# Recurrent mixer: chunk products as single 32x32 blocks in 32-row, 32-column tiles of the array

## The reference, cut to what matters

```python
def step(state, inp):
    r_t, w_t, k_t, v_t, kk_t, a_t = inp
    sa = jnp.einsum('bhvk,bhk->bhv', state, -kk_t)
    state = (state * w_t[:, :, None, :]
             + sa[..., None] * (kk_t * a_t)[:, :, None, :]
             + v_t[..., None] * k_t[:, :, None, :])
    y_t = jnp.einsum('bhvk,bhk->bhv', state, r_t)
    return state, y_t
```

## Time and profile before

| | us |
|---|---|
| median of 3 runs | 3006.22 |
| lowest, highest | 3001.57, 3009.12 |
| the profiled execution | 3007.8 |
| its span | 3006.0 |
| TensorE busy in it | 2891.0 (96%) |
| VectorE busy | 2076.3 (69%) |
| ScalarE busy | 1485.9 (49%) |

### The profile page before, as it was taken

How to read it: one execution, slowest core, us unless ns; L and a number is a source line. 1 busy time by engine, 2 the same in 40 slices (tenths; PEclk the granted TensorE clock), 3 DMA queues, 4 the chain that set the end, 5 groups by cost and what they waited for, 6 DMA issues and landing times.

```text
span 3006.0 us, 57317 instructions
## 1 busy us (share of the span) xinstructions
PE 2891.0 (96%) x24112; PEld 2684.4 (89%) x24112; DVE 2076.3 (69%) x3498; ACT 1485.9 (49%) x2406; POOL 291.1 (10%) x488
## 2 busy tenths in 40 slices
PE   6889999999999999999999998999999999999987
PEld 2578877889998899999899998999999999999987
DVE  6357777687788886756656657575988746887565
ACT  3335555365566646554443433545655444555454
POOL 0012222100133222100000011010000000000000
PEclk8799999999999999999999998999999999999999
DMA  9888877885755566554333333565555555555543
GB/s 388 314 266 265 267 262 242 300 287 176 199 174 166 169 203 196 183 172 156 117 121 118 122 115 118 165 197 183 163 183 185 187 185 179 184 183 188 177 161 113
DMA packets 168210, 580.79 MB, mean 193 GB/s; under 512 B 40273, under 2 KB 40305, under 8 KB 155537
## 3 DMA queue, kind: packets, MB, share of 16 engines
q1 hardware_dynamic: 146784, 525.40, 53.0%
q0 software_dynamic: 20592, 48.26, 5.3%
q10 hardware_dynamic: 576, 3.47, 0.3%
HBM read 555.22 MB, written 21.76 MB: 192 GB/s over the span
## 4 chain that ended last, share of the span: by engine, by line
PE 86%; DMA 5%; DVE 5%; ACT 1%; issue 1%; SPq 1%; POOL 1%; DVEq 0%; ACTq 0%
PE acc L1004 84%; DMA arena<-in_w_ada 2%; DVE arena L972 2%; PE acc L1007 2%; DVE rounded L972 1%; DMA scr_k<-arena 1%; SPq L969 1%; DMA upper<-in_w_ada 1%; DVE upper L972 1%; DVE upper L980 1%; DMA scr_u<-upper 0%; DMA arena<-scr_k 0%; DVE rounded L980 0%; ACT arena L1001 0%; POOL arena L969 0%
## 5 line engine op out<-in xcount | busy, mean ns | idle before, releaser
L1004 PE MATMUL acc<-rounded 128*128 128x256 f32 x14592 | 1883.6, 287 | 20.6 <-issue 9.0
L1004 PEld LDWEIGHTS acc<-rounded 128*128 128x128 f32 x14592 | 1795.7, 193 | 100.4 <-issue 83.0
L1001 ACT ACTIVATE rounded<-arena 128x1024 fp32r<-128x1024 f32 (+1 forms) x862 | 875.3, 1022 | 749.5 <-PE acc L1004 677.1
L972 DVE TENSOR_TENSOR rounded<-arena,rounded 128x1024 fp32r<-128x1024 f32 (+1 forms) x830 | 985.0, 1199 | 260.0 <-ACT rounded L1001 259.5
L1004 PEld LDWEIGHTS acc<-upper_rounded,rounded 128*128 128x128 f32 x4656 | 563.6, 193 | 18.0 <-issue 14.2
L1004 PE MATMUL acc<-upper_rounded,rounded 128*128 128x256 f32 x4656 | 570.2, 284 | 2.7 <-DVE rounded L972 2.0
L1001 ACT ACTIVATE arena<-arena 128x256 f32<-128x256 f32 (+3 forms) x473 | 233.0, 515 | 170.7 <-DVE arena L972 116.1
L972 DVE TENSOR_TENSOR arena<-acc,arena 128x256 f32<-128x256 f32 (+5 forms) x270 | 113.9, 432 | 238.1 <-PE acc L1004 237.3
L972 DVE TENSOR_TENSOR arena<-arena 128x256 f32<-128x256 f32 (+4 forms) x455 | 234.6, 526 | 36.9 <-ACT arena L1001 28.9
L1004 PE MATMUL acc<-arena 128*32 128x512 f32 (+7 forms) x1542 | 214.4, 486 | 39.3 <-DMA arena<-in_w_ada 24.8
L980 DVE SCALAR_TENSOR_TENSOR arena<-arena 128x256 f32<-128x256 f32 (+5 forms) x465 | 205.3, 446 | 29.9 <-ACT arena L1001 21.8
(11 more groups left out here) (92 smaller groups left out, 1212.4 us busy)
## 6 DMA issues: line engine op xcount, KB each, us to landing
arena<-in_w_in SPq DMA_DIRECT2D x328, 512.0 KB, 4.7
arena<-in_w_ada SPq DMA_DIRECT2D x88, 1024.0 KB, 5.2
arena<-in_w_up SPq DMA_DIRECT2D x176, 512.0 KB, 4.0
arena<-in_w_down SPq DMA_DIRECT2D x88, 512.0 KB, 3.8
arena<-in_w_outa SPq DMA_DIRECT2D x32, 512.0 KB, 5.6
arena<-in_w_glu SPq DMA_DIRECT2D x32, 512.0 KB, 5.4
arena<-in_w_outm SPq DMA_DIRECT2D x32, 512.0 KB, 4.8
arena<-in_w_out SPq DMA_DIRECT2D x32, 512.0 KB, 4.0
```

What stands on the lines that cost most here:

```text
L972: return self.put(self.e and self.e.tensor_tensor(o, a, b, op))
L1001: return self.put(self.e and self.e.activation(o, a, f, scale=scale, **kw))
L1004: return self.put(self.e and self.e.matmul(o, l, r, start=start, stop=stop, skip_group_check=True))
```

## The change

The masks shrink from 128 to 32 columns, and each unit's operand from 128 (or 192) columns to 32 (or 96): a chunk's rows stay on their own 32 partitions, and its block begins at column 0. Every product is then made block by block. A tile of 32 rows and 32 columns of the array takes a chunk's block of weights; four chunks of a unit lie on four such tiles along the diagonal.

```diff
-        def four(bank, l, r, n=128):
-            for u in range(4):
-                x = pe.mm(B(bank, 128 * u, n), V(l + 128 * u, 128), V(r + 128 * u, n), True, True)
+        def chunks():
+            return [(u, dict(p0=32 * r, np_=32)) for u in range(4) for r in range(4)]
+
+        def scores(bank, l, r, *dims):
+            for hf in range(2):
+                for c in range(4):
+                    for hd in range(2):
+                        at = 128 * hf + 32 * c
+                        x = pe.mm(B(bank + hd, 128 * hf, 32 * (1 if len(dims) == 1 else 2), p0=32 * c, np_=32),
+                                  V(l + at, 32, p0=64 * hd, np_=64), V(r + at, *dims, p0=64 * hd, np_=64), True, True)
             return x
 
-        def apply(bank, l, src):
-            for u in range(4):
-                x = pe.mm(B(bank, 256 * u, 192), V(l + 128 * u, 128), V(src + 192 * u, 192), True, True)
+        def four(bank, l, r):
+            for u, p in chunks():
+                x = pe.mm(B(bank, 32 * u, 32, **p), V(l + 32 * u, 32, **p), V(r + 32 * u, 32, **p), True, True)
+            return x
+
+        def apply(bank, l, step, src):
+            for u, p in chunks():
+                x = pe.mm(B(bank, 128 * u, 96, **p), V(l + step * u, 32, **p), V(src + 96 * u, 96, **p), True, True)
+            return x
+
+        def rows(at, n, l, step, r, step_r):
+            for hf in range(2):
+                for c in range(4):
+                    for hd in range(2):
+                        u, p = 2 * hd + hf, dict(p0=32 * c, np_=32)
+                        x = pe.mm(B(3 + c, at + 128 * hf, n, p0=64 * hd, np_=64), V(l + step * u, 64, **p),
+                                  V(r + step_r * u, n, **p), True, True)
             return x
```

Steps 4 and 5 use `scores` for `ab`, `ba` and `mrk` (16 products each, where there were 4). Steps 6 to 12 keep their calls of `four` and `apply`, now of 16 products each. In step 13 TensorE has:

```diff
-            for u, (hd, hf) in enumerate(U4):
-                x = pe.mm(B(7, 128 * hf, 128, p0=64 * hd, np_=64), V(QTT + 192 * u, 64), V(MBT + 192 * u, 128), True, True)
-            x.then_inc("rw_pe", ("g7", i))
-            for u in range(4):
-                x = pe.mm(B(4 + u // 2, 256 * (u % 2), 192), V(QTT + 192 * u + 64, 128), V(MBT + 192 * u, 192), True, True)
-            x.then_inc("rw_pe", ("hk", i))
-            for u, (hd, hf) in enumerate(U4):
-                x = pe.mm(B(3, 256 * hf, 256, p0=64 * hd, np_=64), V(QTT + 192 * u, 64), V(BTM + 256 * u, 256), True, True)
-            x.then_inc("rw_pe", ("f", i))
+            apply(7, QTT + 64, 96, MBT).then_inc("rw_pe", ("hk", i))
+            rows(0, 96, QTT, 96, MBT, 96).then_inc("rw_pe", ("gf", i))
```

and in step 14 `e` becomes `rows(0, 64, KE, 64, VTK, 64)`; `y` stays four products of 64-column weights, with its right side in a block-spread copy `MRW`. On ScalarE the moves out of PSUM shrink from 512 to 128 columns (steps 6 to 8) and from 768 to 384 (steps 10, 11). On VectorE:

```diff
-            dve.tt(V(BTM, (256, 4), (64, 4), (1, 64)), V(MBT + 128, (192, 4), (0, 4), (1, 64)),
-                   V(CON + CCOL["ch4"], (0, 4), (1, 4), (0, 64)), MUL)
...
-            dve.tt(V(EE, 512), V(EE, 512), B(5, 0, 512), ADD).then_inc("rw_dve", (e, i))
+            dve.tt(V(EE, 128), V(EE, 128), B(5, 0, 128), ADD).then_inc("rw_dve", (e, i))
...
-            dve.tt(V(QTT, 4, 192), V(QTT, 4, 192), B(3, 0, (256, 4), (1, 192)), ADD).then_inc("rw_dve", ("a3", i))
+            dve.tt(V(QTT, 4, 96), V(QTT, 4, 96), B(3, 0, (128, 4), (1, 96)), ADD).then_inc("rw_dve", ("a3", i))
...
-            dve.wait_ge("rw_pe", ("g7", i))
-            dve.tt(V(G + 256 * i, 256), B(7, 0, 256), V(Rf, 256), ADD)
             dve.wait_ge("rw_pe", ("hk", i))
-            dve.tt(f4(MRK), f4(MRK), quad(4, 0), ADD)
-            dve.wait_ge("rw_pe", ("f", i))
-            dve.tt(V(Bf, 8, 64), B(3, 0, 8, 64), V(CON + CCOL["id64"], (0, 8), (1, 64)), ADD)
+            dve.tt(V(MRK, 4, 32), V(MRK, 4, 32), B(7, 0, (128, 4), (1, 32)), ADD)
             dve.wait_ge("rw_act", ("kv", i))
-            dve.tt(V(KE, 4, 64), V(KTT, 4, 64), B(4, 128, (256, 4), (1, 64)), ADD)
-            dve.tt(V(BTM, (256, 4), (64, 4), (1, 64)), V(VTK, (64, 4), (0, 4), (1, 64)),
-                   V(CON + CCOL["ch4"], (0, 4), (1, 4), (0, 64)), MUL).then_inc("rw_dve", ("vm", i))
+            dve.tt(V(KE, 4, 64), V(KTT, 4, 64), B(7, 32, (128, 4), (1, 64)), ADD)
+            dve.settle()
+            dve.tt(V(MRW, 4, 4, 32), V(MRK, (32, 4), (0, 4), (1, 32)), V(CON + CCOL["ch4"], (0, 4), (1, 4), (0, 32)), MUL)
+            dve.wait_ge("rw_pe", ("gf", i))
+            dve.tt(V(G + 256 * i, 2, 4, 32), B(3, 0, (128, 2), (512, 4), (1, 32)), V(Rf, 2, 4, 32), ADD)
+            dve.tt(V(Bf, 2, 4, 64), B(3, 32, (128, 2), (512, 4), (1, 64)), V(CON + CCOL["id64"], (0, 2), (0, 4), (1, 64)),
+                   ADD).then_inc("rw_dve", ("vm", i))
```

More of the change, by code:

```diff
@@ L68, in const_array @@
     put("chk", np.where(t // 64 <= s // 64, 0, -1e30))
[L69 to L73, removed]
+    i, j = s % 32, np.arange(32)[None, :]
+    put("m16s", (i < j) & (i // 16 == j // 16))
+    put("mo", (i < j) & (i // 16 != j // 16))
+    put("m32i", i <= j)
+    put("m16t", (j < i) & (i // 16 == j // 16))
+    put("m32t", j < i)
+    put("i32", i == j)
     put("scm", np.broadcast_to(np.arange(256) % 32 != 0, (128, 256)))
@@ L121 @@
 CON = _c.alloc(NCON)
+ROOM = _c.alloc(448)
 COS = _c.alloc(256)
@@ L171 @@
 CQ, CQH = Q0T, BTM + 768
+MRW = BTM
 MPR, MPT, MSM, MNM = TMPS + 1024, TMPS + 1408, TMPS + 1792, TMPS + 1800
@@ L229, in mask4 @@
     def mask4(self, name):
-        return self.V(CON + CCOL[name], (0, 4), (1, 128))
+        return self.V(CON + CCOL[name], (0, 4), (1, 32))
     def HT(self, j):
@@ L1300, in rw @@
             pe.wait_ge("rw_dve", ("z", i))
-            for u, (hd, hf) in enumerate(U4):
-                x = pe.mm(B(3 + hd, 256 * hf, 256), half(Bf, hd, hf, 128), half(Af, hd, hf, (256, 2), (1, 128)), True, True)
-            x.then_inc("rw_pe", ("ab", i))
-            for u, (hd, hf) in enumerate(U4):
-                x = pe.mm(B(5 + hd, 256 * hf, 256), half(Af, hd, hf, 128), half(Bf, hd, hf, (256, 2), (1, 128)), True, True)
-            x.then_inc("rw_pe", ("ba", i))
+            scores(3, Bf, Af, (256, 2), (1, 32)).then_inc("rw_pe", ("ab", i))
+            scores(5, Af, Bf, (256, 2), (1, 32)).then_inc("rw_pe", ("ba", i))
             if i:
@@ L1319, in rw @@
             pe.wait_ge("rw_dve", ("m3", i))
-            for u, (hd, hf) in enumerate(U4):
-                x = pe.mm(B(3 + hd, 256 * hf, 128), half(Kf, hd, hf, 128), half(Rf, hd, hf, 128), True, True)
-            x.then_inc("rw_pe", ("mrk", i))
+            scores(3, Kf, Rf, 32).then_inc("rw_pe", ("mrk", i))
             pe.wait_ge("rw_act", ("bt", i))
@@ L1348, in rw @@
             pe.wait_ge("rw_dve", ("e3", i))
-            apply(3, EE, Q0T).then_inc("rw_pe", ("a1", i))
+            apply(3, EE, 32, Q0T).then_inc("rw_pe", ("a1", i))
         if s == 11:
             pe.wait_ge("rw_act", ("a1", i))
-            apply(5, OO, QTT).then_inc("rw_pe", ("a2", i))
+            apply(5, OO, 32, QTT).then_inc("rw_pe", ("a2", i))
         if s == 12:
             pe.wait_ge("rw_act", ("a2", i))
-            apply(3, EE, Q0T).then_inc("rw_pe", ("a3", i))
+            apply(3, EE, 32, Q0T).then_inc("rw_pe", ("a3", i))
         if s == 13:
@@ L1358, in rw @@
             pe.wait_ge("rw_act", ("kv", i))
-            for u, (hd, hf) in enumerate(U4):
-                x = pe.mm(B(7, 128 * hf, 128, p0=64 * hd, np_=64), V(QTT + 192 * u, 64), V(MBT + 192 * u, 128), True, True)
-            x.then_inc("rw_pe", ("g7", i))
-            for u in range(4):
-                x = pe.mm(B(4 + u // 2, 256 * (u % 2), 192), V(QTT + 192 * u + 64, 128), V(MBT + 192 * u, 192), True, True)
-            x.then_inc("rw_pe", ("hk", i))
-            for u, (hd, hf) in enumerate(U4):
-                x = pe.mm(B(3, 256 * hf, 256, p0=64 * hd, np_=64), V(QTT + 192 * u, 64), V(BTM + 256 * u, 256), True, True)
-            x.then_inc("rw_pe", ("f", i))
+            apply(7, QTT + 64, 96, MBT).then_inc("rw_pe", ("hk", i))
+            rows(0, 96, QTT, 96, MBT, 96).then_inc("rw_pe", ("gf", i))
         if s == 14:
             pe.wait_ge("rw_dve", ("vm", i))
+            rows(0, 64, KE, 64, VTK, 64).then_inc("rw_pe", ("e", i))
             for u, (hd, hf) in enumerate(U4):
[L1371 to L1374, removed]
+                x = pe.mm(B(7, 128 * hf, 128, p0=64 * hd, np_=64), V(VTK + 64 * u, 64), V(MRW + 128 * u, 128), True, True)
             x.then_inc("rw_pe", ("y", i))
@@ L2264, in rw @@
         Af, Bf = AR + 512 * i, BK + 512 * i
-        quad = lambda bank, off: B(bank, off, (256, 4), (1, 128))
-        f4 = lambda base: V(base, 4, 128)
+        quad = lambda bank, off: B(bank, off, (512, 2), (128, 2), (1, 32))
+        f4 = lambda base, step=32: V(base, (2 * step, 2), (step, 2), (1, 32))
+        mask = lambda name: V(CON + CCOL[name], (0, 2), (0, 2), (1, 32))
         if s == 1:
@@ L2299, in rw @@
             dve.wait_ge("rw_pe", ("ab", i))
[L2300 to L2302 removed]
+            dve.tt(f4(DD), quad(3, 0), mask("m16s"), MUL)
+            dve.tt(f4(OO), quad(3, 0), mask("mo"), MUL)
+            dve.tt(f4(MBT, 96), quad(3, 32), mask("m32i"), MUL).then_inc("rw_dve", ("m3", i))
             dve.wait_ge("rw_pe", ("ba", i))
[L2304 to L2307 removed]
```

(5 more changed lines are left out.)

33 lines of the change are left out of this document (11 added, 22 removed).

## The result

| | before | after |
|---|---|---|
| median, us | 3005.66 (3001.57 to 3009.12) | 2940.44 (2932.61 to 2943.78) |
| ratio, 95% interval | | 0.9783 [0.9769, 0.9796] |
| the profiled execution | 3007.8 | 2932.6 |
| its span | 3006.0 | 2930.8 |
| groups of the mixer begin every (mean of seven) | 51.40 | 43.76 |

The account below looks back on a forecast made before the run. TensorE was taken to bound the mixer. Waves 7.7, borders 4.0 and instruction supply 0.5 make 12.2 us a group against 19.0: 54 us for eight, 55 with step 10's wait, off 3007.8 gives 2953 us; range 2938 to 3014.

Parts of the forecast that it names:

- The bound: Mixer's eight groups: TensorE bounds them, so its savings come off the end one for one; VectorE's and ScalarE's hardly count.
- Step 10's old wait: Step 10 stands 0.27 us for step 9's VectorE addition; shorter additions mostly end it, worth 1 us over all groups.
- named signs of being wrong: Granted clock below 1.00 in the stage, borders far over 0.33 us, or VectorE or ScalarE waits at steps 5, 10, 14.
- The waves: Small-tile products of a group: 7.7 us in all, a four-tile wave of `four` at 0.045 us (0.031 to 0.062).
- Step 9: Step of one `four` call: 32 records, about 0.4 to 0.5 us from its start to the next dense record.
- The borders: Changes of tile shape: 0.33 us for each of eleven blocks a group, 0.2 for each change inside steps 13 and 14; 4.0.
- The supply of instructions: Bursts in the mixer that outrun the supply of instructions: 0.5 us a group (0 to 1.5).
- The sum: One mixer group falls from 19.0 to 12.2 us: 6.8 saved, 54 us for eight groups.
- this case's own low end: Whole kernel: low end of the main forecast's range, 2941 to 2972 us, from savings of 4.5 to 8.3 a group.
- Rival 1: `four` and `apply`: row tiles sharing a PSUM bank take turns, 5.9 us more a group, 3055 us; chance 0.12.
- Rival 2: Mixer's small tiles: each record costs a floor of 0.027 us whatever its size, no change, 3009 us; chance 0.13.
- Rival 3: Steps 6 to 12: instructions come too slowly, 0.024 us each, half the gain, 2980 us; chance 0.13.

Follow-up runs that it names:

- moves_twice: The changed kernel with every move out of PSUM in steps 4 to 13 on ScalarE and every masked multiply or addition on VectorE made twice: 2940.80 us.
- after_again: The changed kernel with nothing altered, measured again: 2941.35 us, ratio to before 0.9790.
- borders experiment: The changed kernel with four more whole-array products a group, between calls of `four` in steps 6, 7 and 8: 2947.99 us.
- own_banks: The changed kernel with step 9's four row tiles writing to four banks and VectorE's addition behind it split in four: 2951.32 us (one run).
- tile_order: The changed kernel with the loop turned so that `four` and `apply` issue one tile's four products in a row: 2995.34 us.
- double_four: The changed kernel with each product of `four` issued twice, 256 more records a group: 2998.34 us.
- phase: The changed kernel with 32 more 32x32 products (128 instructions) in step 0 of group 1: 2933.64 us (one run).
- merged_spread: The changed kernel with two dense slots moved from behind step 5 to behind steps 6 and 7, and `mrk` made in step 4: 2931.79 us.

## Why the prediction was right, and where it was off

**The bound.** Right. TensorE had the stage, its time came off the end one for one (62.2 of the 75 us between the profiled executions lie in the stage), and moves_twice puts back most of ScalarE's part and under half of VectorE's without any cost. No new wait came up at steps 5, 10 or 14. Step 10's old wait of 0.27 is gone in most groups; the 1 us for it is too small a term to tell. One of the named signs of being wrong did show, though not for the reason given: the granted clock fell in the stage of after_again, behind a gap and not because the tiles are small; in the profile of after it stayed at 1.00 through all of them.

**The waves.** Mis-sized. I took 0.045 us for a wave of `four`, halfway between 0.031 and 0.062. Step 9 takes 0.38, of which 8 x 0.033 = 0.26 are waves, and each further call in a block costs 0.30, 0.037 a wave. For 64 waves that is 2.2 us, not 2.9. The lower bound from the loads in the earlier trace rows was the truth. With 32 columns streamed in both, the records of one tile start 58 to 59 ns apart in the 64x64 tiles of `rw_seq` and 32 to 33 in `mrk` with its 64 rows by 32 columns of weights: half the weights' columns, about half the time. At 32x32 the streamed columns alone would be 27 ns, so load and stream are not told apart there. With the fixed parts the four steps of `four` were priced at 3.8 us start to start and took 2.71; an `apply` at 0.91, taken 0.80; `mrk` at 0.46, taken 0.29; step 13 at 1.5, taken 1.32; step 14 at 1.17, taken 1.01.

**The borders.** The total of 0.33 for each holds, its parts do not. The way in costs more than my 0.09: twelve dense products took 1.62 where 12 x 0.12 is 1.44, so 0.18. The way out with what is fixed in the block costs less than my 0.13 + 0.10: 0.38 - 0.26 = 0.12. That makes 0.30, and the borders experiment sets 0.40 as the upper bound. I had set before's borders (1.06) against the ways in of after (1.0), as if they were the same; in fact the ways in grew by 0.8 us a group.

**The supply of instructions.** The term was there (0.5, from 0 to 1.5), its mechanism was not. I had thought of a rate. What came are single stops at every 256th instruction that falls into a block of small tiles: 1.1 to 2.7 us in four groups, 0 to 0.5 of smaller losses in the others, 1.2 a group on average.

**The sum.** Without stops 8.8 us a group came off where I had 7.3 and the wait of step 10: the blocks gave 2.1 more than I had (8.5 for 10.6 without their ways in), the ways in took 0.8 back, and the wait gave 0.27. With the stops it is 7.6 a group (51.40 - 43.76) where I had 6.8. For the stage that is 62 us in place of 55, inside the 36 to 66 that the bounds gave. The times themselves end just under this case's own low end of 2941: the median at 2940.44, and the profiled execution, for which the sum was made, at 2932.6, as 13 us more came off where the change touches nothing. The mechanism held; the term that was mis-sized most is the waves.

**Rival 1** falls. `four` and `apply` take a quarter of its price with all four row tiles in one bank, and own_banks shows no difference with four banks. The rule in the Trainium skill, "TensorEngine Tiling (Array Packing)", section "Restrictions and Gotchas", that row tiles cannot use one bank at once, does not hold for tiles that write to different partitions: 0.38 us by either arrangement. tile_order shows what waiting for one another looks like, on one tile of the array and not on a bank: 0.82.

**Rival 2** falls. 8.75 ns a record, not 27. The distance of 0.031 in `rw_seq` was the load. The figure of 25 ns in the Trainium skill, "TensorE: Matmul & The Clock Gate", section "Wait — 56ns, not 53.3ns?", agrees with one tile (27 to 35 ns in tile_order) and not with several: the four records of a wave start about 7 ns apart.

**Rival 3** fell as it was put (0.024 us an instruction; 4.1 to 4.7 ns were reached), and was right in kind. double_four, with only 256 records more a group, lost 23 us to gaps and 15 to 17 to the clock: the change lies close to where this rival decides.

## What to carry to other kernels

Small tiles pay on Trainium2 if neighbouring products in the program lie on different tiles: the order of the loop was worth 54 of the change's 65 us. They are cheap in array time and dear in instructions, so look for gaps that are put down to issue, count the instructions up to each, and put dense products between bursts of small ones; a gap costs its length, and sometimes as much again or more in clock (3.4 us beside one of 2.4). Price a block of small tiles amid dense products as 0.3 to 0.4 us for the borders and, at 32x32, 0.033 to 0.037 us for a wave of four.

## What the runs showed of the hardware

- **Instruction fetch.** Instructions come in packets of 256. A block of 32x32 products uses them at 4.1 to 4.7 ns each (8.3 to 9.4 ns a record with its load), and then the packet's arrival, 2.2 us after its start, shows: gaps of 0.9 to 2.5 us at one place in 256, up to 3.8 with 192 records in a row. The Trainium skill, "Runtime: NRT & Kernel Launch", section "Instruction fetch mechanics", describes the blocks of 256 instructions, and the traces agree; it holds the fetch to be hidden, as instructions are dispatched more slowly than they come, and there they disagree.
- **The clock after a gap.** In or behind gaps of TensorE of 1.5 to 3.8 us the clock in some cases fell to 1.2 GHz for a few us: at 2.38 us in after_again, at 1.81, 1.58 and 1.52 in own_banks, at 2.11 and 2.17 in phase, at 2.10 in merged_spread, and seven times in the groups of double_four. In others not: 2.52 us in after, 2.21 in moves_twice, 1.87 in own_banks and 1.82 in after_again left it at 2.4 GHz. Nothing here tells the two apart.
- **Row tiles and banks.** Four row tiles write into one bank at once, if their partitions differ (0.38 us a step with one bank or four).
- **Order of issue.** Four products in a row on the same 32x32 tile follow each other, and about two tiles work at a time where the diagonal order has four: 0.82 against 0.38 us for 32 records, 1.88 against 0.80 with 96 columns.
